# A decoder layer in one kernel: dots that read tokens from SBUF, squares of the norms summed on three engines, and a later hand-over of the low halves

## The chip, the cores and the metric

The kernel runs on one core of one Trainium2 chip. The metric is the device time of one execution in microseconds. Three runs of the kernel before took 3889.0 to 3893.97 us, with a median of 3889.63.

## What is computed

One layer on x with 512 tokens and 2048 channels, in float32. The reference, cut:

```python
proj = x @ w_in[i]
y_conv = conformer_conv(a_conv, ...)      # GLU, causal depthwise conv(31), LayerNorm over 1024, silu, matmul
y_attn = diff_attention(q, k, v, ...)     # 8 heads
mixed = gates[:, :, 0] * y_conv + gates[:, :, 1] * y_attn
x = layer_norm(ALPHA * x + mixed @ w_out[i], ln1_g[i], ln1_b[i])
x = layer_norm(ALPHA * x + peer(x, ...), ln2_g[i], ln2_b[i])
x = x + sigmoid(x @ w_pg + b_pg) * (p[i] @ w_p)
```

and in `peer`, for each token and each of 8 heads, 16 of 16384 experts are picked by product keys:

```python
u = u_tab[ids]
v = v_tab[ids]
h = gelu(einsum('td,thkd->thk', xb, u))
w = (g * h)
return einsum('thk,thkd->td', w, v)
```

## The kernel before

**Layout.** Activations lie transposed: partitions are channels within a chunk of 128, the free axis is tokens. Every large product is a matmul of a 128 x 128 weight tile with 512 (or 352) token columns. To keep float32 accuracy each operand is split in a high half of the type fp32r and a low half, and `three` (lines 655 to 659) issues three matmuls: high x high, low activation x high weight, high activation x low weight.

**Weights.** They come as 784 blocks of 128 x 1024 (512 KB), two of which are a unit. SyncE loads them into four buffers `raw`, ScalarE copies each to `whi` (`hi_part`, L1031) once TensorE is done with the block four before it (AHEAD = 4), and a third engine makes `wlo = raw - whi`: GpSimd in `lo_part` (L570) or VectorE in `lo_part` (L1606). TensorE's `one_block` waits on `lo_done` and then issues 24 matmuls. A raw buffer is loaded again when its low half is made.

**Stages, in blocks.** Heads and gates (B1, B1T), branch outputs (B2), w_out (B3), norm 1, expert queries (B4, 32 blocks), the expert-up loop U5 (B5, 256 blocks, 64 steps of 4), the expert-down loop U6 (B6, 256 blocks), norm 2, and the last projections (B7, B8).

**Two ways through the experts.** For tokens 0 to 351 the kernel runs all 16384 experts densely (352 columns, TU) and keeps the gates in DRAM (`expert_spill`), which is zeroed first and then written one gate per partition by scattered writes: `put_gate` (L592), 384 of them, each after `sum_gate` on VectorE (L1628) has summed the gates of equal experts. For the last 160 tokens it gathers the picked rows: 160 rows per partition of `u_tab` (`gather_u`, L612) and then of `v_tab` (L638), 1 MB for each gather, into a ring of four buffers. `put_gates(n)` stands behind gather n in GpSimd's program, 2.56 writes for each n from 6 on. The first 32 rows (NXP) belong to 32 extra tokens, four times over the partitions. VectorE takes the dot of a gathered row with the token: `extra_dot` (L1619) for the first 32 against `x1e` in SBUF, and `dot` (L1612) for the other 128 against `quad` in PSUM, where TensorE has put the last 128 tokens by sixteen transposes.

**The order on VectorE.** Before the expert-up loop it does the top-16 searches and the routing (decode, weights, offsets). During the first PRE = 7 steps of the loop it is still in its routing and GpSimd makes the low halves, up to DVE_LO = B5 + 4 * PRE. Then VectorE waits for `lo_done` of DVE_LO, makes two lows ahead (LEAD) and runs six `expert_tile`s of 32 blocks: a low, the gate sums, and in three of four blocks a dot. What is left is `POST_DOTS`: 16 dots in the first 20 of 36 blocks.

**The norms.** `norm` on VectorE subtracts the mean of each chunk, `norm_squares` on ScalarE (L1047) squares it into one of two buffers, and `norm_var` on TensorE (L700) sums the squares over partitions and chunks with a matrix of ones: 8 for the conv norm, 16 each for norms 1 and 2. ScalarE waits for the sum of two squares earlier before it writes a buffer again. After the last one ScalarE takes the root (L1050), VectorE the reciprocal, and the chunks are scaled one by one. For the conv norm this stands in TensorE's program behind block 7 of B1T, with blocks 8 to 15 behind it.

Of the kernel before, what the change touches and what calls it, by code (L numbers as in the profile page):

```python
# [18 lines left out]
P = 128  # L19
# [3 lines left out]
ALU = mybir.AluOpType  # L23
# [54 lines left out]

PRE = 7

# [45 lines left out]
def build(nc, ws, xT, pT, cpar, pvec, lamT, keysT, u_tab, v_tab, out):  # L126
# [6 lines left out]
    with ExitStack() as ctx:  # L133
# [28 lines left out]

        x1e = at("x1e", o_ahi, [P, KD, T])

        urows = at("urows", o_s, [P, RING, D])
# [73 lines left out]
        c[0] = o_phase  # L239
        sq = small("sq", [P, 2, T])  # L240
        std = small("std", [P, T])
# [4 lines left out]
        c[0] = o_after_ln  # L246
        gl = small("gl", [P, 2, 2, T])
        mt = small("mt", [P, T])
        xr = small("xr", [P, 2, T])

# [56 lines left out]

        msum2 = at("msum2", o_after_ln, [P, T])
        o_p = c[0]
        c[0] = o_p  # L310
# [53 lines left out]

        ln = [{n: sem(f"{n}{i}") for n in ("mean", "cent", "sqr", "sqr_used", "std_ok", "scaled", "affine", "hi_ok", "lo_ok", "sum")} for i in range(3)]

# [23 lines left out]
        x1e_full = sem("x1e_full")  # L390
        x1e_ok = sem("x1e_ok")
        xsrc_ok = sem("xsrc_ok")
        xg_in = sem("xg_in")
# [152 lines left out]
        def _(pool):  # L546
# [26 lines left out]
            def lo_parts(first, n):  # L573
                with pool.Fori(0, n // 4) as i:
                    for s in range(4):
                        lo_part(4 * i + (first + s), s)

            def spread_picks():

                pool.wait_ge(xsrc_ok, 1)  # L580
                for j in range(NJ):
                    pool.dma_start(xg[j * NX:(j + 1) * NX], xsrc[P - NX:P, :, j * NXP:(j + 1) * NXP]
                                   ).then_inc(xg_in, 16)
# [57 lines left out]

            lo_parts(0, DVE_LO)
            spread_picks()
# [5 lines left out]
            pool.wait_ge(lo_done, B7)  # L649
            lo_parts(B7, NB - B7)  # L650


        @block.tensor
        def _(pe):
# [41 lines left out]
            def norm_var(i, n):  # L696
                for k in range(n):

                    pe.wait_ge(ln[i]["sqr"], k + 1)
                    mm = pe.matmul(ps_o[:], ones[:], sq[:, k % 2], start=(k == 0), stop=(k == n - 1))  # L700
                    mm.then_inc(ln[i]["sqr_used"], 1)

# [94 lines left out]
            for n in range(2 * U1T):  # L797
# [9 lines left out]
                if n == 7:  # L807
                    norm_var(0, NH)

# [214 lines left out]
        def _(act):  # L1024
# [13 lines left out]
            def norm_squares(i, n, src):  # L1038

                act.activation(std[:, 0:1], eps[:], ACT.Sqrt)  # L1040
                for k in range(n):

                    act.wait_ge(ln[i]["cent"], k + 1)
                    if k >= 2:

                        act.wait_ge(ln[i]["sqr_used"], k - 1)
                    act.activation(sq[:, k % 2], src[:, k], ACT.Square).then_inc(ln[i]["sqr"], 1)  # L1047

                act.wait_ge(ln[i]["sqr_used"], n)
                act.activation(std[:], ps_o[:], ACT.Sqrt, bias=eps[:], scale=1.0 / (n * P)  # L1050
# [171 lines left out]
            act.copy(x1e[:, :, TD:T], quad[:].rearrange("p (k d) -> p k d", k=KD)).then_inc(x1e_ok, 1)  # L1222
            with act.Fori(1, SOFT) as i:
                expert_step(i)
# [99 lines left out]
        def _(dve):  # L1324
# [89 lines left out]
            def norm(i, n, src, after):  # L1414
                dve.drain().then_inc(ln[i]["sum"], 1)
                dve.wait_ge(ln[i]["mean"], 1)
                for k in range(n):
                    dve.scalar_tensor_tensor(src[:, k], ps_x[:], -1.0 / (n * P), src[:, k],
                                             ALU.mult, ALU.add).then_inc(ln[i]["cent"], 1)
                dve.wait_ge(ln[i]["std_ok"], 1)  # L1420
                dve.reciprocal(rstd[:], std[:])
# [187 lines left out]
            def dot(n, m, s):  # L1609

                dve.wait_ge(rows_in[s], 16 * m + 16)
                dve.scalar_tensor_tensor(urows[:, s], urows[:, s], 1.0, quad[:], ALU.mult, ALU.mult,  # L1612
                                         accum_out=hd[:, bass.ds(n, 1)]).then_inc(rows_used, 1)
# [40 lines left out]
            dve.wait_ge(x1e_ok, 2)  # L1654
            dve.wait_ge(x1t_full, 1)

# [223 lines left out]
```

## Time and profile before

| | |
|---|---|
| median of 3 runs | 3889.63 us |
| profiled execution | 3876.91 us |
| its span, first to last instruction | 3875.1 us |
| TensorE matmul busy | 3708.9 us (96%) |
| VectorE busy | 2570.0 us (66%) |
| GpSimd busy | 1653.4 us (43%) |
| ScalarE busy | 1296.8 us (33%) |
| mean granted clock of TensorE | 0.976 |
| DMA | 873.53 MB, 225 GB/s over the span |

Busy time is the sum of an engine's instructions; for a stretch of the span the same is given with the clock that TensorE was granted there. A bracket behind an instruction tells how long its engine was idle before it and what ended that. PE is TensorE, PEld its weight loads, ACT ScalarE, DVE VectorE, POOL GpSimd, SP SyncE. Times of instructions are counted from the start of the span.

### The profile page before, as it was taken

Reading aid. Unit: us, or ns where it says so; the run is one execution under the profiler, and the core shown is the slowest. Engines: PE = TensorE matmul, PEld = TensorE weight load, DVE = VectorE, ACT = ScalarE, POOL = GpSimd, SP = SyncE. Lnnn points to the kernel's source line nnn. Section 1 sums busy time; section 2 is a strip of 40 time slices with the busy share of each in tenths; the row PEclk is TensorE's granted clock in tenths of the full one; section 3 lists DMA queues with packets and bytes.
Section 4 is the critical chain, followed back from the end, with each engine's and each line's share of the span. In section 5 each row is a group of like instructions: output and inputs, shape, how many; then the busy total and the mean of one; then the engine's idle time right before and its main releaser. Section 6 shows DMA issues by size and latency. Waiting matters only on the chain.

```text
span 3875.1 us, 56496 instructions
## 1 busy us (share of the span) xinstructions
PE 3708.9 (96%) x19704; PEld 3339.5 (86%) x19704; DVE 2570.0 (66%) x4070; ACT 1296.8 (33%) x1665; POOL 1653.4 (43%) x1032
## 2 busy tenths in 40 slices
PE   8999999999998999898999988999999999999999
PEld 6888888878886889897888887889999999999777
DVE  3555555544413679866777776756999999999732
ACT  4443334441213324343322222223333333333442
POOL 4444444434443336586666565521332222223143
PEclk9999999999999999898999998999999999999999
DMA  5433343324433224788888787877999999999332
GB/s 187 130 125 127 125 129 125 124 98 139 152 121 100 83 91 149 278 298 293 302 313 290 274 301 269 283 261 276 380 385 363 354 362 352 360 358 348 126 111 74
DMA packets 245800, 873.53 MB, mean 225 GB/s; under 512 B 35600, under 2 KB 76752, under 8 KB 204624
## 3 DMA queue, kind: packets, MB, share of 16 engines
q1 hardware_dynamic: 154864, 496.64, 38.1%
q0 software_dynamic: 59360, 340.13, 23.2%
q10 hardware_dynamic: 31488, 35.66, 2.5%
q8 instruction: 47, 0.77, 0.1%
q14 instruction: 41, 0.34, 0.0%
HBM read 813.38 MB, written 58.90 MB: 225 GB/s over the span
## 4 chain that ended last, share of the span: by engine, by line
PE 82%; DVE 7%; issue 4%; POOL 4%; DVEq 2%; ACT 1%; DMA 1%; ACTq 0%; SPq 0%; POOLq 0%
PE bank L657 26%; PE bank L659 26%; PE bank L658 26%; POOL expert_spill L592 3%; DVE yx L1720 2%; PE quad L700 1%; DVE sc L1393 1%; DVE pick L1558 1%; POOL urows L612 1%; DVE wlo L1606 1%; PE bank L719 1%; DVEq L1559 1%; DVEq L1682 0%; PE quad L747 0%; PE bank L858 0%
## 5 line engine op out<-in xcount | busy, mean ns | idle before, releaser
L657 PE MATMUL bank<-ahi,whi 128*128 128x352 f32 (+1 forms) x3968 | 1446.3, 364 | 85.3 <-issue 33.9
L1031 ACT ACTIVATE whi<-raw 128x1024 fp32r<-128x1024 f32 x784 | 827.3, 1058 | 2078.6 <-PE bank L659 1294.9
L659 PE MATMUL bank<-ahi,wlo 128*128 128x352 f32 (+1 forms) x3968 | 1433.9, 361 | 28.8 <-issue 27.7
L658 PE MATMUL bank<-alo,whi 128*128 128x352 f32 (+1 forms) x3968 | 1432.4, 361 | 29.0 <-issue 27.7
L570 POOL TENSOR_TENSOR wlo<-raw,whi 128x1024 fp32r<-128x1024 f32 x304 | 752.0, 2477 | 1056.8 <-ACT whi L1031 1044.0
L657 PEld LDWEIGHTS bank<-ahi,whi 128*128 128x128 f32 x3968 | 763.0, 192 | 191.3 <-issue 78.4
L659 PEld LDWEIGHTS bank<-ahi,wlo 128*128 128x128 f32 x3968 | 762.8, 192 | 122.7 <-issue 45.0
L658 PEld LDWEIGHTS bank<-alo,whi 128*128 128x128 f32 x3968 | 762.7, 192 | 114.3 <-issue 42.0
L1606 DVE TENSOR_TENSOR wlo<-raw,whi 128x1024 fp32r<-128x1024 f32 x484 | 590.1, 1220 | 281.5 <-ACT whi L1031 211.7
L657 PE MATMUL bank<-xwhi,whi 128*128 128x352 f32 x2048 | 661.4, 323 | 1.3 <-DVE xwlo L1692 0.6
L658 PE MATMUL bank<-xwlo,whi 128*128 128x352 f32 x2048 | 656.2, 320 | 0.0
L659 PE MATMUL bank<-xwhi,wlo 128*128 128x352 f32 x2048 | 656.2, 320 | 0.0
L592 POOL DMA_INDIRECT expert_spill<-gval,goff x384 | 431.6, 1124 | 140.0 <-issue 115.2
L638 POOL DMA_INDIRECT vrows<-v_tab,idx x128 | 205.4, 1605 | 547.5 <-DVE yacc L1708 491.8
L657 PEld LDWEIGHTS bank<-xwhi,whi 128*128 128x128 f32 x2048 | 384.1, 188 | 2.7 <-DVE wlo L1606 1.5
L658 PEld LDWEIGHTS bank<-xwlo,whi 128*128 128x128 f32 x2048 | 385.1, 188 | 0.0
L659 PEld LDWEIGHTS bank<-xwhi,wlo 128*128 128x128 f32 x2048 | 384.0, 187 | 0.0
L1612 DVE SCALAR_TENSOR_TENSOR urows<-urows,quad 128x2048 f32<-128x2048 f32 x128 | 292.1, 2282 | 9.2 <-DMA urows<-u_tab,idx 4.9
L1708 DVE SCALAR_TENSOR_TENSOR yacc<-vrows,hd,yacc 128x2048 f32<-128x2048 f32 x116 | 273.4, 2357 | 25.0 <-issue 23.6
L1393 DVE SCALAR_TENSOR_TENSOR sc<-glu,cur,sc 128x512 f32<-128x512 f32 x232 | 270.2, 1165 | 17.3
L612 POOL DMA_INDIRECT urows<-u_tab,idx x128 | 155.4, 1214 | 207.3 <-DVE urows L1612 173.8
L1243 ACT ACTIVATE xwhi<-wt 128x352 fp32r<-128x352 f32 x120 | 59.8, 498 | 336.7 <-DVE wt L1687 329.5
(231 smaller groups left out, 2596.2 us busy)
## 6 DMA issues: line engine op xcount, KB each, us to landing
raw<-ws SPq DMA_DIRECT2D x788, 512.0 KB
hg<-expert_spill SPq DMA_DIRECT2D x58, 704.0 KB, 9.2
expert_spill<-zero SPq DMA_DIRECT2D x32, 704.0 KB, 5.9
expert_spill<-hst ACTq DMA_DIRECT2D x128, 176.0 KB
gate_spill<-gout ACTq DMA_DIRECT2D x32, 256.0 KB, 2.0
gl<-gate_spill SPq DMA_DIRECT2D x32, 256.0 KB, 2.7
expert_spill<-gval,goff POOLq DMA_INDIRECT x384
hg<-expert_spill POOLq DMA_DIRECT2D x6, 704.0 KB, 4.7
```

The lines of the kernel that those rows point to most:

```text
L570: nc.gpsimd.tensor_tensor(wlo[:, s], raw[:, s // 2, s % 2], whi[:, s].bitcast(F32), ALU.subtract).then_inc(lo_done, 1)
L592: nc.gpsimd.indirect_dma_start(eg_flat, bass.IndirectOffsetOnAxis(ap=goff[here, a, n:n + 1], axis=0), gval[here, a, n:n + 1], None).then_i ...
L612: nc.gpsimd.indirect_dma_start(urows[:, n % RING], None, u_tab, bass.IndirectOffsetOnAxis(ap=at_col, axis=0)).then_inc(rows_in[n % RING], 16)
L638: nc.gpsimd.indirect_dma_start(vrows[:, n % RING], None, v_tab, bass.IndirectOffsetOnAxis(ap=at_col, axis=0)).then_inc(rows_in[n % RING], 16)
L657: pe.matmul(ps_out, hi, xh, start=first, stop=False)
L658: pe.matmul(ps_out, hi, xl, start=False, stop=False)
L659: return pe.matmul(ps_out, lo, xh, start=False, stop=last)
L1031: act.activation(whi[:, s], raw[:, s // 2, s % 2], ACT.Copy).then_inc(hi_done, 1)
L1393: dve.scalar_tensor_tensor(dst, glu[:, w:w + T], cur[:, w:w + 1], acc, ALU.mult, ALU.add)
L1606: dve.tensor_tensor(wlo[:, s], raw[:, s // 2, s % 2], whi[:, s].bitcast(F32), ALU.subtract).then_inc(lo_done, 1)
L1612: dve.scalar_tensor_tensor(urows[:, s], urows[:, s], 1.0, quad[:], ALU.mult, ALU.mult, accum_out=hd[:, bass.ds(n, 1)]).then_inc(rows_used, 1)
L1708: dve.scalar_tensor_tensor(yacc[:], vrows[:, s], w, yacc[:], ALU.mult, ALU.add).then_inc(rows_used, 1)
```

## The change

Three edits. PRE goes from 7 to 8. The tokens of the dots are copied from PSUM to `x1t` in SBUF by ScalarE after step 1 of the expert-up loop, and `dot` reads them there. The squares of norms 1 and 2 go in turn to `sqe`, whose column sums TensorE still takes, and to `sqo`, which GpSimd adds up in `sqsum` (`sum_squares`, between two stretches of its low halves); TensorE takes one column sum of that at the end. For the conv norm VectorE adds up all eight squares, and TensorE takes one column sum (`conv_var`).

```diff
-PRE = 7
+PRE = 8
...
+        x1t = at("x1t", o_alo, [P, KD, T])
...
+            def sum_squares(i, n):
+
+                for k in range(1, n, 2):
+                    pool.wait_ge(ln[i]["sqr"], k + 1)
+                    this = sqo[i][:, k // 2 % 2]
+                    if k == 1:
+                        ad = nc.gpsimd.tensor_copy(sqsum[i][:], this)
+                    else:
+                        pool.drain()
+                        ad = nc.gpsimd.tensor_tensor(sqsum[i][:], sqsum[i][:], this, ALU.add)
+                    ad.then_inc(ln[i]["sqr_sum"], 1)
...
-            lo_parts(0, DVE_LO)
+            lo_parts(0, B4 + AHEAD)
+            sum_squares(1, KD)
+            lo_parts(B4 + AHEAD, DVE_LO - B4 - AHEAD)
...
             pool.wait_ge(lo_done, B7)
-            lo_parts(B7, NB - B7)
+            lo_parts(B7, AHEAD)
+            sum_squares(2, KD)
+            lo_parts(B7 + AHEAD, NB - B7 - AHEAD)
...
             def norm_var(i, n):
-                for k in range(n):
+                for k in range(0, n, 2):
 
                     pe.wait_ge(ln[i]["sqr"], k + 1)
-                    mm = pe.matmul(ps_o[:], ones[:], sq[:, k % 2], start=(k == 0), stop=(k == n - 1))
-                    mm.then_inc(ln[i]["sqr_used"], 1)
+                    pe.matmul(ps_o[:], ones[:], sqe[:, k // 2 % 2], start=(k == 0), stop=False
+                              ).then_inc(ln[i]["sqr_used"], 1)
+                pe.wait_ge(ln[i]["sqr_sum"], n // 2)
+                pe.matmul(ps_o[:], ones[:], sqsum[i][:], start=False, stop=True).then_inc(ln[i]["sqr_used"], 1)
+
+            def conv_var():
+
+                pe.wait_ge(ln[0]["sqr_sum"], NH)
+                pe.matmul(ps_o[:], ones[:], sqsum[0][:], start=True, stop=True).then_inc(ln[0]["sqr_used"], 1)
...
                 if n == 7:
-                    norm_var(0, NH)
+                    conv_var()
...
                     act.wait_ge(ln[i]["cent"], k + 1)
-                    if k >= 2:
-
-                        act.wait_ge(ln[i]["sqr_used"], k - 1)
-                    act.activation(sq[:, k % 2], src[:, k], ACT.Square).then_inc(ln[i]["sqr"], 1)
-
-                act.wait_ge(ln[i]["sqr_used"], n)
+                    if i == 0 and k >= 2:
+                        act.wait_ge(ln[i]["sqr_sum"], k - 1)
+                    elif k >= 4:
+                        act.wait_ge(ln[i]["sqr_sum" if k % 2 else "sqr_used"], k // 2 - 1)
+                    to = sqe[:, k % 2] if i == 0 else (sqo[i] if k % 2 else sqe)[:, k // 2 % 2]
+                    act.activation(to, src[:, k], ACT.Square).then_inc(ln[i]["sqr"], 1)
+
+                act.wait_ge(ln[i]["sqr_used"], 1 if i == 0 else n // 2 + 1)
...
-            with act.Fori(1, SOFT) as i:
+            expert_step(1)
+
+            act.wait_ge(x1t_full, 1)
+            act.copy(x1t[:, :, TD:T], quad[:].rearrange("p (k d) -> p k d", k=KD)).then_inc(x1t_ok, 1)
+            with act.Fori(2, SOFT) as i:
                 expert_step(i)
...
+                if i == 0:
+                    for k in range(n):
+                        dve.wait_ge(ln[i]["sqr"], k + 1)
+                        if k == 0:
+                            ad = dve.tensor_copy(sqsum[0][:], sqe[:, 0])
+                        else:
+                            dve.drain()
+                            ad = dve.tensor_tensor(sqsum[0][:], sqsum[0][:], sqe[:, k % 2], ALU.add)
+                        ad.then_inc(ln[i]["sqr_sum"], 1)
                 dve.wait_ge(ln[i]["std_ok"], 1)
...
-                dve.scalar_tensor_tensor(urows[:, s], urows[:, s], 1.0, quad[:], ALU.mult, ALU.mult,
+                rows = urows[:, s].rearrange("p (k d) -> p k d", k=KD)
+                dve.scalar_tensor_tensor(rows, rows, 1.0, x1t[:, :, TD:T], ALU.mult, ALU.mult,
                                          accum_out=hd[:, bass.ds(n, 1)]).then_inc(rows_used, 1)
...
-            dve.wait_ge(x1t_full, 1)
+            dve.wait_ge(x1t_ok, 1)
```

On GpSimd, this is the place between the loop of the low halves and the gathers, before (the four rows in front are the end of that loop, whose count is not in them):

```order
L570 TENSOR_TENSOR wlo<-raw,whi 128x1024
L574 REGISTER_ALU
L574 COMPARE_AND_BRANCH
L582 DMA xg<-xsrc 32x2x32 x4
L612 DMA urows<-u_tab,xg 128x2048 x7
L592 DMA expert_spill<-gval,goff 11534336x1 x3
```

and now (L576 is the low half, L590 and L593 are `sum_squares` for norm 1, L600 the picks, L630 a gather, L610 a scattered write):

```order
L576 TENSOR_TENSOR wlo<-raw,whi 128x1024
L580 REGISTER_ALU
L580 COMPARE_AND_BRANCH
L590 COPY sqsum_155<-sqo_152 128x512
L593 TENSOR_TENSOR sqsum_155<-sqsum_155,sqo_152 128x512 x7
L580 UNCONDITIONAL_BRANCH
...
L576 TENSOR_TENSOR wlo<-raw,whi 128x1024
L580 REGISTER_ALU
L580 COMPARE_AND_BRANCH
L600 DMA xg<-xsrc 32x2x32 x4
L630 DMA urows<-u_tab,xg 128x2048 x7
L610 DMA expert_spill<-gval,goff 11534336x1 x3
```

The loop is cut in two around one copy and seven adds, and the second part runs to four blocks later before the picks and gathers.

On VectorE, the conv norm before:

```order
L1418 SCALAR_TENSOR_TENSOR conv<-quad,conv 128x512 x8
L1421 RECIPROCAL rstd<-std 128x512
L1428 TENSOR_TENSOR nrm<-conv,rstd 128x512 x2
L1436 TENSOR_TENSOR swlo<-conv,swhi 128x512
```

and now:

```order
L1453 SCALAR_TENSOR_TENSOR conv<-quad,conv 128x512 x8
L1459 COPY sqsum_154<-sqe 128x512
L1462 TENSOR_TENSOR sqsum_154<-sqsum_154,sqe 128x512 x7
L1465 RECIPROCAL rstd<-std 128x512
L1472 TENSOR_TENSOR nrm<-conv,rstd 128x512 x2
L1480 TENSOR_TENSOR swlo<-conv,swhi 128x512
```

A copy and seven adds came between the centring of the eight chunks and the reciprocal.

## Rows read from the trace of the kernel before

**Rows 1.** Stretches: busy time and count of each engine, granted clock, DMA share, GB/s.
```profile
core 0: us, PE busy (x) PEld busy (x) DVE busy (x) ACT busy (x) POOL busy (x), PEclk, DMA share, GB/s
1658.00:1758.00 100.00, 91.05 (x541) 89.31 (x541) 70.63 (x134) 41.24 (x44) 82.63 (x58) 0.97 0.89 299
1758.00:2552.00 794.00, 698.79 (x3836) 655.82 (x3835) 541.87 (x1019) 213.08 (x254) 474.03 (x442) 0.91 0.83 289
```

**Rows 2.** Timeline of POOL before the hand-over: start, length, instruction, idle before.
```profile
1530.30 2.39 POOL L570 TENSOR_TENSOR wlo<-raw,whi 128x1024 fp32r<-128x1024 f32 x1 [1.38 <-ACT whi L1031]
...
1545.77 2.39 POOL L570 TENSOR_TENSOR wlo<-raw,whi 128x1024 fp32r<-128x1024 f32 x1 [1.21 <-ACT whi L1031]
...
1552.92 1.04 POOL L612 DMA_INDIRECT urows<-u_tab,xg  x1 [2.38 <-DMA xg<-xsrc]
```

**Rows 3.** Timeline of PE at the hand-over.
```profile
1577.87 0.66 PE L657 MATMUL bank<-ahi,whi 128*128 128x352 f32 x1 [17.82 <-DVE wlo L1606]
```

**Rows 4.** Timeline of DVE behind the last dot.
```profile
2582.59 1.23 DVE L1606 TENSOR_TENSOR wlo<-raw,whi 128x1024 fp32r<-128x1024 f32 x1 [0.16 <-ACT whi L1031]
...
2598.06 1.23 DVE L1606 TENSOR_TENSOR wlo<-raw,whi 128x1024 fp32r<-128x1024 f32 x1 [2.55 <-ACT whi L1031]
```

**Rows 5.** Timeline of DVE and POOL: a dot from SBUF, one from PSUM.
```profile
1653.86 2.29 DVE L1619 SCALAR_TENSOR_TENSOR urows<-urows,x1e 128x2048 f32<-128x2048 f32 x1 [3.26 <-DMA urows<-u_tab,xg]
1653.92 3.08 POOL L592 DMA_INDIRECT expert_spill<-gval,goff  x1 [0.30 <-issue]
...
1772.34 2.28 DVE L1612 SCALAR_TENSOR_TENSOR urows<-urows,quad 128x2048 f32<-128x2048 f32 x1
1773.03 0.97 POOL L592 DMA_INDIRECT expert_spill<-gval,goff  x1 [0.30 <-issue]
```

**Rows 6.** Instructions of one line: least, median and greatest ns.
```profile
L1222 ACT COPY x1e<-quad x1: 1870/1870/1870, 1465.7 to 1465.7; 128x2048 f32<-128x2048 f32 x1
L1468 DVE TENSOR_TENSOR msum<-msum,res x15: 691/691/693, 1075.1 to 1227.5; 128x512 f32<-128x512 f32 x15
```

**Rows 7.** POOL by groups, 1658 to 1758 and 1758 to 2552: busy, mean ns, idle.
```profile
L592 POOL DMA_INDIRECT expert_spill<-gval,goff x41 | 66.5, 1622 | 12.5 <-issue 12.5
L612 POOL DMA_INDIRECT urows<-u_tab,xg x16 | 16.8, 1048 | 4.9 <-issue 4.9
...
L592 POOL DMA_INDIRECT expert_spill<-gval,goff x317 | 324.2, 1023 | 119.6 <-issue 94.7 <-DMA expert_spill<-gval,goff 20.9 <-DVE same L1628 3.9
L612 POOL DMA_INDIRECT urows<-u_tab,idx x125 | 151.6, 1213 | 200.7 <-DVE urows L1612 167.2 <-issue 33.6
```

**Rows 8.** Timeline of POOL: gathers 8, 16, 24, 32 and 156.
```profile
1604.67 2.34 POOL L612 DMA_INDIRECT urows<-u_tab,xg  x1 [0.30 <-issue]
...
1657.30 0.97 POOL L612 DMA_INDIRECT urows<-u_tab,xg  x1 [0.30 <-issue]
...
1708.38 0.97 POOL L612 DMA_INDIRECT urows<-u_tab,xg  x1 [0.30 <-issue]
...
1757.95 0.97 POOL L612 DMA_INDIRECT urows<-u_tab,idx  x1 [0.30 <-issue]
...
2551.78 1.95 POOL L612 DMA_INDIRECT urows<-u_tab,idx  x1 [0.66 <-issue]
```

**Rows 9.** The matches for the gate writes: least, median and greatest ns.
```profile
L1628 DVE SCALAR_TENSOR_TENSOR same<-gflat,gone x384: 227/292/354, 1580.2 to 2524.8; 128x16 f32<-128x16 f32 x24, 128x32 f32<-128x32 f32 x24, 128x48 f32<-128x48 f32 x24, 128x64 f32<-128x64 f32 x24
```

**Rows 10.** Timeline of ACT: first squares and std of conv norm, norm 1, norm 2.
```profile
819.80 1.14 ACT L1047 ACTIVATE sq<-conv 128x512 f32<-128x512 f32 x2
...
830.20 0.69 ACT L1050 ACTIVATE std<-quad,eps 128x512 f32<-128x512 f32 x1 [1.22 <-PE quad L700]
...
1230.18 1.23 ACT L1047 ACTIVATE sq<-res 128x512 f32<-128x512 f32 x2 [0.99 <-DVE res L1418]
...
1246.22 0.69 ACT L1050 ACTIVATE std<-quad,eps 128x512 f32<-128x512 f32 x1 [1.22 <-PE quad L700]
...
3644.25 1.23 ACT L1047 ACTIVATE sq<-res 128x512 f32<-128x512 f32 x2 [5.32 <-DVE res L1418]
...
3661.91 0.69 ACT L1050 ACTIVATE std<-quad,eps 128x512 f32<-128x512 f32 x1 [1.22 <-PE quad L700]
```

More of the change, by code:

```diff
@@ L239, in build @@
         c[0] = o_phase
-        sq = small("sq", [P, 2, T])
+        sqe = small("sqe", [P, 2, T])
         std = small("std", [P, T])
@@ L247, in build @@
         gl = small("gl", [P, 2, 2, T])
+        o_mt = c[0]
         mt = small("mt", [P, T])
+        o_xr = c[0]
         xr = small("xr", [P, 2, T])
@@ L308, in build @@
         msum2 = at("msum2", o_after_ln, [P, T])
+        sqo = [sqe, at("sqo1", o_xr, [P, 2, T]), at("sqo2", o_after_ln + 4 * KB, [P, 2, T])]
+        sqsum = [at("sqsum0", o_mt, [P, T]), at("sqsum1", o_mt, [P, T]), at("sqsum2", o_after_ln + 2 * KB, [P, T])]
         o_p = c[0]
@@ L363, in build @@
         gate_out = [sem(f"gate_out{i}") for i in range(2)]
-        ln = [{n: sem(f"{n}{i}") for n in ("mean", "cent", "sqr", "sqr_used", "std_ok", "scaled", "affine", "hi_ok", "lo_ok", "sum")} for i in range(3)]
+        ln = [{n: sem(f"{n}{i}") for n in ("mean", "cent", "sqr", "sqr_used", "sqr_sum", "std_ok", "scaled", "affine", "hi_ok", "lo_ok", "sum")} for i in range(3)]
         evac2 = sem("evac2")
@@ L391, in build @@
         x1e_ok = sem("x1e_ok")
+        x1t_ok = sem("x1t_ok")
         xsrc_ok = sem("xsrc_ok")
```

## The prediction

> **What bounds the kernel now.** The busy shares come first: TensorE is busy 96% of the span, so a gain must come from stretches where it is not. The stretch table by time finds them. From 1758 to 2552 us, where 124 of the 160 expert rows per token are gathered, TensorE is busy 699 of 794 us at a granted clock of 0.91 and DMA is at 0.83 [rows 1]. That is the expert-up loop (256 weight blocks of 352 columns). Beside each block VectorE makes the low half, and beside three of four blocks it makes one dot of a gathered row, while GpSimd issues 2.56 scattered gate writes for each gather. Two things are to be seen ahead of it. VectorE is still busy with the routing when it has to take over the low halves: GpSimd's lows come every 3.87 us (four in 1545.77 - 1530.30 = 15.47 us) and stop with block 27 [rows 2]; TensorE then stands 17.8 us for VectorE's first low [rows 3]. And at each of the three layer norms TensorE does little: 16 us of squares and column sums, one bound to the next.
>
> **Part 1, PRE 7 to 8.** GpSimd keeps four more low halves (blocks 28 to 31 of the loop). The routing on VectorE is not touched and ends at the same 1576.6. TensorE does these four blocks in 15.5 us of its 17.8 us of standing, and waits about 2.4 us instead. The gain stays if what follows keeps its rate: dots are bound to blocks by the program, all of it shifted by four blocks, so that at the last dot (about 2580 us) 12 blocks are left, not 16. Blocks without dots go at 3.87 us (2582.59 to 2598.06 for four [rows 4]): **-15.5 us**. GpSimd's first gather has to wait for its last low, some 15.5 us later than 1552.9 [rows 2], so 1568.4; VectorE waits for the picks that come before that gather, and is still in its routing until 1576.6. The first two gathers have 8 us left to land. I cost this at nothing; if that cover were gone, it would cost the few us by which the picks are late.
>
> **Part 2, dots from SBUF.** The dot does not get faster: 2.29 us with x1e in SBUF, 2.28 with the tokens in PSUM [rows 5]. The added ScalarE copy is like the one of x1e, 1.87 us [rows 6], beside three blocks of prepared weights: nothing. What changes is GpSimd. With an SBUF dot on VectorE, an indirect DMA that starts 0.06 us behind the dot takes 3.08 us; in a PSUM dot one takes 0.97 [rows 5]. The first 32 dots already read SBUF, so the kernel before shows both. In the stretch with SBUF dots a scattered write takes 1.622 us on average and GpSimd is never idle but for 0.30 us of issue; afterwards 1.023 us, and GpSimd waits 167 us for dots [rows 7]. So GpSimd loses its slack of 167 us and becomes the engine that sets the pace of the loop. How fast? From gather 16 to gather 32 (1657.30 to 1757.95) 6.29 us each; from 32 to 156 (to 2551.78), 6.40 each [rows 8]. The other way round, the 442 instructions of that stretch at the SBUF prices are 317 x 1.622 + 125 x 1.048 + 442 x 0.30 = 778 us, against 794 now. The matches that VectorE does for the gate writes also hold SBUF, and grow from 0.23 to 0.35 us over the loop [rows 9], 2.56 of them for each gather: on average of the later rows 0.055 us wider than in the measured stretch, so at most 0.14 us a gather or 17 us in all, and I take half, 9. That makes 787: **-7 us**. Why a slower GpSimd need not lengthen the loop: now it runs ahead at 1.28 us a transfer whenever a buffer comes free, then waits; VectorE waits for weights in that stretch while TensorE stands. Bounds: 778 with no growth (-16); the whole SBUF window (gather 8 to 32, 153.3 us, 6.39 each) with all the growth, 792 + 17 (+15).
>
> The Trainium skill, page "SBUF — State Buffer", section "Who interferes with whom", says that a VectorE instruction with two SBUF inputs contends with a GpSimd instruction that reads SBUF, but infers that descriptor generation is left alone, as it needs the write interface. Here the indirect DMAs, which read their indices from SBUF, do stretch, so the trace agrees with the first half and speaks against the second. By the second half alone part 2 would be worth nothing and the time 3866.
>
> **Part 3, the norms.** Conv norm: the squares start at 819.80 and the std at 830.20 [rows 10], because the eight column sums wait behind block 7. Now VectorE adds: an add of this size is 0.69 us [rows 6], 0.77 with the drain, so the eighth is in at about 820.4 + 0.5 + 7 x 0.77 = 826.3, and with 1.2 us for the one column sum std starts at 827.5: -2.7. TensorE now stands about 3.5 us there; should the clock fall, it eats this. I take -2.5. Norm 1: 1230.18 to 1246.22, 16.0 us; norm 2: 3644.25 to 3661.91, 17.7 us [rows 10]. Now ScalarE can go at its 0.62 us a square (two in 1.23), 10 us in all, TensorE sums the even ones, and GpSimd adds the odd ones. Its add is not in the trace. Below: half the 2.39 us of its low of twice the size [rows 2], 1.2, and with drain and semaphore 1.4, so 1.3 + 0.9 + 7 x 1.4 + 1.2 = 13.2 us. Above: 2.4 us each regardless of size, 22 us. A tensor operation of the same kind is most likely in proportion; I take 13.9 us. That is -2.1 and -3.8, and the recipes behind (reciprocal, scaling) are unchanged. TensorE has nothing queued but the blocks that need this norm. **-8.4 us**; if GpSimd's add cost 2.4 us each, norms 1 and 2 would give +10 instead of -6.
>
> **Sum:** -15.5 - 7 - 8.4 = **-31 us**. Against the profiled execution (3876.9, span 3875.1) 3846; against the median of the three timed runs, 12.7 us above it, **3859**. I carry the same difference over to the median.
>
> **Rivals.**
> 1. *GpSimd's pace is worse than the loop's now* (slower). Deciding point: the gains besides it are 24 us, so 124 gathers must take over 818 us, 6.59 us each. For it: eight gathers of the SBUF stretch took 6.58 (1604.67 to 1657.30); against it: the next eight 6.39, the next 6.20, falling [rows 8]. At 6.58 and with the whole 17 us of growth, 833: +39, in all 3889.6 - 24 + 39 = 3905. 10%.
> 2. *Given back* (same): 6.58 without growth is 816, +22, leaving 3888; or GpSimd's adds at 2.4 us, 3875, with some of the pace lost too. 10%.
> 3. *No contention felt* (faster, by the part 2 that is worth nothing): the ring of four buffers already hid GpSimd, the loop stays at 6.40 a gather: -24, 3866. 15%.
> 4. *The loop runs more evenly* (faster): the last eight SBUF gathers took 6.20; 124 at that are 769, -25 in place of -7, and the stalls of TensorE between 1758 and 2552 fall away: 3841. 15%.
> That the change does not do what it says is excluded for the dots and lows, which are plain in the order; for the norms it would be rival 2.
>
> **Numbers.** The forecast has 50%. Faster by over 0.2% (7.8 us, about what a measurement of this kernel tells from no change) holds with the forecast and rivals 3 and 4 and the better part of rival 2's second half: 0.81. Same 0.10, slower 0.09. The range leaves out rival 1 and the far end of 4: 3838 to 3889.
>
> **What would show it.** TensorE's stand at the takeover 2 to 4 us, not 17.8. GpSimd's scattered writes at 1.6 us on average through the whole loop, its wait for dots near zero, gathers 6.2 to 6.5 us apart. From the first square to std 7.7, 13.9 and 13.9 us. The prediction is wrong if gathers are over 6.59 us apart, if TensorE stands over 10 us at the takeover for another reason (picks late), or if a sum on GpSimd takes over 2 us.

## The result and the profile after

| | before | change |
|---|---|---|
| median of 4 runs | 3889.32 us | 3837.77 us |
| lowest and highest | 3877.72, 3893.97 | 3833.62, 3845.64 |
| profiled execution | 3876.91 us | 3838.33 us |
| mean granted clock | 0.976 | 0.985 |

The ratio is 0.9874, 95% interval 0.9847 to 0.9901: 51.6 us by the medians, 38.6 us by the two profiled executions. The forecast was 3859, faster, with a range from 3838; the median lies 0.2 us below its low end. This is the result beside one set of runs of the kernel before. Beside another set (2, below) the change is slower than before by 3.6%; the experiments come to that.

The page after, its span, busy shares and chain (before, the chain had PE 82% and POOL 4%):

```profile
span 3836.5 us, 56450 instructions
PE 3656.1 (95%) x19662; PEld 3320.2 (87%) x19662; DVE 2581.6 (67%) x4074; ACT 1301.0 (34%) x1668; POOL 1827.5 (48%) x1052
...
PE 63%; POOL 19%; DVE 7%; issue 5%; DVEq 2%; DMA 1%; ACT 1%; ACTq 0%; POOLq 0%; SPq 0%
```

The loop's two stretches after, gather 16 to 32 (1661.7 to 1762.6) and gather 32 to 156, in the columns of [rows 1]:

```profile
1663.00:1763.00 100.00, 93.27 (x556) 91.82 (x555) 70.00 (x136) 41.86 (x44) 82.63 (x58) 0.97 0.91 300
1763.00:2541.00 778.00, 674.46 (x3951) 656.00 (x3950) 553.07 (x1023) 219.92 (x261) 617.45 (x442) 0.96 0.88 298
```

The same 442 instructions of GpSimd that took 474 us of 794 now take 617 of 778. The groups of GpSimd and VectorE in that second stretch (compare [rows 7]):

```profile
L610 POOL DMA_INDIRECT expert_spill<-gval,goff x317 | 476.7, 1504 | 122.7 <-issue 95.1 <-DMA expert_spill<-gval,goff 24.1 <-DVE same L1673 3.6
L630 POOL DMA_INDIRECT urows<-u_tab,idx x125 | 141.8, 1135 | 38.1 <-issue 38.1
...
L1657 DVE SCALAR_TENSOR_TENSOR urows<-urows,x1t 128x2048 f32<-128x2048 f32 x123 | 281.9, 2292 | 206.0 <-DMA urows<-u_tab,idx 164.3 <-issue 41.3
```

GpSimd never waits for a dot any more (167 us before). The wait has changed sides: VectorE's dots now wait 164 us for gathered rows (4.9 us before). GpSimd sets the pace.

The hand-over after, on GpSimd, TensorE's weight loads and VectorE (compare [rows 2] and [rows 3]):

```profile
1560.04 2.40 POOL L576 TENSOR_TENSOR wlo<-raw,whi 128x1024 fp32r<-128x1024 f32 x1 [1.48 <-ACT whi L1060]
1562.38 2.44 POOL L600 DMA_DIRECT2D xg<-xsrc  x4
1567.30 1.04 POOL L630 DMA_INDIRECT urows<-u_tab,xg  x1 [2.48 <-DMA xg<-xsrc]
...
1585.15 0.29 PEld L679 LDWEIGHTS bank<-ahi,whi 128*128 128x128 f32 x1 [11.11 <-DVE wlo L1650]
...
1583.85 3.51 DVE L1650 TENSOR_TENSOR wlo<-raw,whi 128x1024 fp32r<-128x1024 f32 x3 [0.31 <-issue]
```

TensorE still stands 11.1 us by its loads, 10.8 by its matmuls (17.8 before), not 2 to 4. VectorE takes over at 1583.85; before it did at 1576.6. Where those 7.3 us come from, two groups of VectorE's routing show, of before from 1545 to 1577:

```profile
L1549 DVE SCALAR_TENSOR_TENSOR term<-pij,know 128x256 f32<-128x256 f32 x30 | 11.4, 421 | 1.1
L1558 DVE TENSOR_TENSOR pick<-pick,term 128x256 f32<-128x256 f32 x30 | 11.4, 421 | 1.5 <-issue 0.4
```

and of after from 1545 to 1584:

```profile
L1602 DVE TENSOR_TENSOR pick<-pick,term 128x256 f32<-128x256 f32 x30 | 20.0, 706 | 1.1
L1593 DVE SCALAR_TENSOR_TENSOR term<-pij,know 128x256 f32<-128x256 f32 x30 | 11.4, 422 | 1.5 <-issue 0.4
```

The thirty adds of `pick`, with two inputs in SBUF, grew by 8.6 us in all. They now lie beside four more low halves of GpSimd. A low half, and two adds of which the first lies beside it:

```profile
1556.17 2.39 POOL L576 TENSOR_TENSOR wlo<-raw,whi 128x1024 fp32r<-128x1024 f32 x1 [1.38 <-ACT whi L1060]
...
1556.36 2.81 DVE L1602 TENSOR_TENSOR pick<-pick,term 128x256 f32<-128x256 f32 x2
```

Only four adds grew: each began 0.05 to 0.3 us behind one of the four low halves, ended just behind it, and took 2.48 to 2.63 us; the others stayed near 0.42. The instructions of `term`, which also read two tensors in SBUF, did not grow: none of them began while a low half ran. The one of the same line that writes `pick` did begin behind one in both kernels, and took 2.48 us before and 2.62 after.

**The account.** These are marks in the two traces, after minus before, with what each stretch gave in brackets: first low half of the expert-up loop -1.1 us; third gather +7.2 (1583.8 against 1576.6; +8.3, the hand-over's loss); gather 32 +4.6 (-2.6); gather 156 -11.1 (-15.7); last dot -20.9 (2559.2 against 2580.1, -9.8); first low of the down loop -40.4 (2608.2 against 2648.6, -19.5); end -38.6 (+1.8).

### The profile page after: what moved, and what is told of

Read it like the earlier page. It is cut to its first block, busy times and chain, and to the rows that moved or that the text cites. A ratio compares the mean times of both kernels' runs of the same rounds, so it can differ in the third digit from the quotient of the medians.

```text
span 3836.5 us, 56450 instructions
## 1 busy us (share of the span) xinstructions
PE 3656.1 (95%) x19662; PEld 3320.2 (87%) x19662; DVE 2581.6 (67%) x4074; ACT 1301.0 (34%) x1668; POOL 1827.5 (48%) x1052
## 4 chain that ended last, share of the span: by engine, by line
PE 63%; POOL 19%; DVE 7%; issue 5%; DVEq 2%; DMA 1%; ACT 1%; ACTq 0%; POOLq 0%; SPq 0%
PE bank L679 20%; PE bank L681 20%; PE bank L680 20%; POOL expert_spill L610 15%; POOL urows L630 4%; DVE yx L1765 2%; DVE sc L1428 1%; DVEq L1603 1%; DVE pick L1602 1%; DMA expert_spill<-gval,goff 1%; DVE wlo L1650 1%; PE bank L748 1%; DVEq L1727 0%; PE quad L776 0%; DMA urows<-u_tab,idx 0%
## 5 line engine op out<-in xcount | busy, mean ns | idle before, releaser
L576 POOL TENSOR_TENSOR wlo<-raw,whi 128x1024 fp32r<-128x1024 f32 x308 | 764.5, 2486 | 1024.7 <-ACT whi L1060 1011.7
L610 POOL DMA_INDIRECT expert_spill<-gval,goff x384 | 579.4, 1509 | 143.2 <-issue 115.5
L1657 DVE SCALAR_TENSOR_TENSOR urows<-urows,x1t 128x2048 f32<-128x2048 f32 x128 | 293.3, 2292 | 210.5 <-DMA urows<-u_tab,idx 168.5
L630 POOL DMA_INDIRECT urows<-u_tab,idx x128 | 145.4, 1136 | 40.8 <-issue 38.7
```

Source lines behind the costliest of these rows:

```text
L576: nc.gpsimd.tensor_tensor(wlo[:, s], raw[:, s // 2, s % 2], whi[:, s].bitcast(F32), ALU.subtract).then_inc(lo_done, 1)
L610: nc.gpsimd.indirect_dma_start(eg_flat, bass.IndirectOffsetOnAxis(ap=goff[here, a, n:n + 1], axis=0), gval[here, a, n:n + 1], None).then_i ...
L630: nc.gpsimd.indirect_dma_start(urows[:, n % RING], None, u_tab, bass.IndirectOffsetOnAxis(ap=at_col, axis=0)).then_inc(rows_in[n % RING], 16)
L1657: dve.scalar_tensor_tensor(rows, rows, 1.0, x1t[:, :, TD:T], ALU.mult, ALU.mult, accum_out=hd[:, bass.ds(n, 1)]).then_inc(rows_used, 1)
```

## The experiments

All times are medians; "before" is the kernel before, run in the same set. A set of runs shares one chip. There were five sets after the result, each with a number here, and the kernel before falls on two levels in them, which are called the lower (3714 to 3718) and the upper (3871 to 3889, the result's own set among them):

| set | kernels | before |
|---|---|---|
| 1 | b_again, b_pre8, b_x1t, b_norms | 3870.6 (3856.3 to 3886.7, 29 runs) |
| 2 | after_again, a_psum, a_paced, a_pre9 | 3718.4 (3701.3 to 3723.2, 13 runs) |
| 3 | a_psum_2, a_ring3 | 3713.9 (3705.1 to 3721.1, 19 runs) |
| 4 | a_half | 3716.1 (3706.1 to 3717.7, 7 runs) |
| 5 | a_psum9 | 3879.2 (3866.4 to 3890.2, 13 runs) |

### The kernel before, unchanged

> The kernel before, unchanged, for its spread. Theory (GpSimd's bursts): the expert-up loop's pace depends on how transfers collide, so the gathers' pace should differ from execution to execution: 6.40 us a gather in the profile of before (3876.9), about 6.5 where an execution takes 3889. Rival: the 12 us between that profile and the median lie anywhere, and the pace is 6.40 again.

Measured 3869.04, ratio 0.9995 [0.9977, 1.0013]. The same program, built again, gives the same time. Gathers 32 to 156 came 6.38 us apart in an execution of 3879, so the theory's 6.5 did not come and the rival's 6.40 did.

### One part alone

```diff
-PRE = 7
+PRE = 8
```

> Before with PRE = 8 alone. Theory (the longer low halves on GpSimd block VectorE's routing): the routing ends 7 to 9 us later, TensorE stands some 11 us at the hand-over, the time falls by 7 to 10 us. Rival (the routing was late by chance): it ends at the old time, TensorE stands 2 to 3 us, -15.5 us.

Measured 3861.84, ratio 0.9974 [0.9954, 0.9994], -9 us. The third gather came at 1588.5 (1577.2 in b_again, whose lows ran 2.5 us earlier); TensorE stood 11.0 us. So the late routing belongs to this part, and it brings what is left of 15.5 us after it. The profiled execution, 3841.91, was the quickest of its ten, and its gathers came 6.20 us apart, so its trace is not that of its median, and the pace of the loop with dots from PSUM is perhaps less steady than b_again alone would say.

```diff
+            act.copy(x1t[:, :, TD:T], quad[:].rearrange("p (k d) -> p k d", k=KD)).then_inc(x1t_ok, 1)
...
-                dve.scalar_tensor_tensor(urows[:, s], urows[:, s], 1.0, quad[:], ALU.mult, ALU.mult,
+                dve.scalar_tensor_tensor(rows, rows, 1.0, x1t[:, :, TD:T], ALU.mult, ALU.mult,
```

> Before with the dots from SBUF alone (and the copy). Theory (the held port keeps GpSimd from bursting, and the loop runs evenly): writes 1.5 us on average, gathers 6.27 us apart, TensorE's clock in the loop up from 0.91 to 0.96, -25 us against the profile of before, up to -38 against its median. Rival (nothing gained here, the gain of the change came from the other two parts): -7 us or less.

Above is the main part of the edit; it also moves ScalarE's step 1 out of its loop, as in the change. Measured 3850.59, ratio 0.9936 [0.9914, 0.9959], -20 us: the largest part by itself. Gathers 32 to 156 came 6.26 us apart. In its groups from 1763 to 2400 GpSimd's writes are as slow as in the change:

```profile
L594 POOL DMA_INDIRECT expert_spill<-gval,goff x264 | 397.2, 1505 | 90.0 <-issue 79.8 <-DMA expert_spill<-gval,goff 10.1
L659 PE MATMUL bank<-ahi,whi 128*128 128x352 f32 x1098 | 368.8, 336 | 75.4 <-DVE wlo L1612 75.1
```

The norms alone (the `sqe`, `sqo`, `sqsum`, `sum_squares` and `conv_var` lines of the diff):

> Before with the new sums of squares alone. Theory (TensorE, left with less work, falls to the low clock, and GpSimd is late in norm 2): -1 to -3 us in all. The forecast: -8.4 us. In norm 2 GpSimd's first add comes 4.8 us late if that is a fixed property of the program, and about 0.2 us late if it was chance.

Measured 3871.53, ratio 0.9994 [0.9972, 1.0015]: nothing that can be told. In its profile, from first square to std: 9.0, 13.7 and 17.7 us (10.4, 16.0 and 16.0 in b_again beside it). GpSimd's first add of norm 2 is 4.8 us late here too.

The three parts alone add up to some 28 us. The change took 51.6 off the medians of its own set and 33 off this set's; its whole was not run in this set, so whether the parts help each other is not shown.

### The change again, and the source of the dots undone

> The change, unchanged, as the base of this group: about 0.990 of the kernel before, the routing late and TensorE's stand at the hand-over 10.8 us again (a fixed property), GpSimd's first add of norm 2 late by 4.8 us again or not.

Measured 3848.82 with before at 3718.4: ratio 1.0358 [1.034, 1.0375], **slower** by 130 us. No theory expected that. But the change itself hardly moved: its four times, 3834 to 3852, overlap with the result's 3834 to 3846, gathers 32 to 156 came 6.25 us apart (6.28 in the result), and TensorE's stand at the hand-over was 10.8 us again. What moved is the kernel before.

```diff
-                dve.scalar_tensor_tensor(rows, rows, 1.0, x1t[:, :, TD:T], ALU.mult, ALU.mult,
+                dve.scalar_tensor_tensor(urows[:, s], urows[:, s], 1.0, quad[:], ALU.mult, ALU.mult,
```

> The change with the dots read from PSUM again (the copy to SBUF stays and is not read). Theory (GpSimd's bursts): gathers 6.3 to 6.5 us apart, DMA uneven, 15 to 25 us slower than the change. Rival (the even pace does not matter): within 5 us of it.

Measured 3708.24, ratio 0.9975 [0.9961, 0.999]; 141 us under the change, by the source of the dots alone. Gathers came 5.17 us apart. It was run again in set 3:

> The changed kernel with its dots reading PSUM again (the copy is made all the same), a second time, beside a new set of the kernel before. If this chip is of the kind on which the kernel before takes 3856 to 3894: theory 1 (the dots from SBUF bring the larger part of the gain there, as b_x1t against before, some 20 us) expects 3852 to 3862, gathers 6.2 to 6.4 us apart and TensorE with issue gaps inside blocks of the up loop. Theory 2 (the hand-over and the norms bring it and the source of the dots is worth nothing) expects 3835 to 3845. If the chip is of the kind on which before takes 3718: 3708 again, gathers 5.17 us apart and no such gaps.

Measured 3703.57, ratio 0.9972 [0.9957, 0.9986]. Its stretch from 1763 to 2400 (columns as in [rows 1]), and its matmul and GpSimd groups there:

```profile
1763.00:2400.00 637.00, 632.52 (x3923) 631.33 (x3922) 547.28 (x1021) 218.03 (x260) 468.46 (x440) 1.00 0.98 362
...
L680 PE MATMUL bank<-alo,whi 128*128 128x352 f32 x1308 | 424.3, 324 | 0.0
L679 PE MATMUL bank<-ahi,whi 128*128 128x352 f32 x1307 | 422.3, 323 | 4.5 <-DVE wlo L1650 4.3
L610 POOL DMA_INDIRECT expert_spill<-gval,goff x315 | 335.2, 1064 | 125.1 <-issue 94.2 <-DMA expert_spill<-gval,goff 30.7 <-DVE same L1672 0.3
```

TensorE is busy 632.5 of 637 us at clock 1.00. Three dots go with four blocks at 3.87 us [rows 4], which is 5.16 us a gather: TensorE's own pace. GpSimd's writes are at 1.06 us and leave it room. The same stretch of the kernel before, as it was profiled for the result:

```profile
1763.00:2400.00 637.00, 564.50 (x3126) 531.81 (x3125) 443.46 (x845) 174.53 (x207) 388.34 (x360) 0.92 0.84 293
...
L659 PE MATMUL bank<-ahi,wlo 128*128 128x352 f32 x1042 | 351.9, 338 | 21.8 <-issue 21.0
L657 PE MATMUL bank<-ahi,whi 128*128 128x352 f32 x1042 | 351.6, 337 | 29.4 <-issue 25.8 <-DVE wlo L1606 2.8
```

Here TensorE has "issue" gaps inside blocks: it waits for nothing that the profile shows. Matmuls that follow each other at 0.16 us elsewhere come 0.7 us apart, in clusters mostly 25 to 50 us from each other; one cluster in windows and in PE's timeline:

```profile
1900.00:1904.00 4.00, 4.00 (x27) 4.00 (x26) 3.91 (x8) 1.57 (x3) 3.35 (x3) 1.00 0.53 148
1912.00:1916.00 4.00, 4.00 (x27) 4.00 (x26) 1.44 (x2) 0.76 (x1) 3.09 (x4) 1.00 1.03 410
1916.00:1920.00 4.00, 2.40 (x9) 1.14 (x7) 3.58 (x6) 0.30 (x1) 3.09 (x4) 1.00 0.98 379
1920.00:1924.00 4.00, 2.77 (x8) 1.94 (x9) 0.39 (x2) 0.00 (x0) 3.09 (x4) 0.64 0.82 259
1924.00:1928.00 4.00, 3.41 (x12) 3.24 (x12) 0.32 (x1) 1.41 (x2) 0.80 (x1) 0.51 0.54 203
...
1917.99 0.41 PE L657 MATMUL bank<-ahi,whi 128*128 128x352 f32 x1 [0.39 <-issue]
1918.70 0.32 PE L658 MATMUL bank<-alo,whi 128*128 128x352 f32 x1 [0.30 <-issue]
```

The gaps begin with DMA at its full share; the granted clock falls after them (1.00, 0.64, 0.51), and DMA then drops to half. The gaps (60 to 72 us of 637 in the three matmul lines) are in every profile with dots from PSUM of sets 1 and 5 and in that of the kernel before, and in none of sets 2 and 3. Profiles with dots from SBUF have none, in any set, but for 10.4 us on one matmul line of the change. In windows of 4 us from 1900 to 2020 the DMA share swings between 0.53 and 1.07 before and 0.71 and 1.01 after; in a_psum_2 it stays at 0.81 to 1.09 without any gap, so a full share by itself does not make them. Nor do loads of instructions, by their number: the trace of before has 10 of them in the 637 us, that of a_psum_2 has 13, and the clusters are some 19.

### Is it GpSimd's pace?

```diff
+                    if NXP <= n < 140:
+                        pool.drain()
+                        nc.gpsimd.memset(idle[:], 0.0)
```

> As a_psum (dots from PSUM), but GpSimd writes a scratch tile for some 0.9 us after the gate writes of each gather from 32 to 139, which with issue and drain makes up the 1.3 to 1.4 us that an SBUF dot holds it. Theory (it is GpSimd's pace that counts, not where the dot reads): the time of the change within 5 us, gathers about 6.3 us apart, GpSimd's wait for dots small. Rival (a PSUM read by VectorE slows TensorE, and SBUF is better in itself): the time of a_psum or worse.

Measured 4201.26, ratio 1.1311 [1.129, 1.1333]. It misses its aim: the edit was to cost 0.9 us a gather, and gathers came 9.16 us apart. The group of the added instruction, from 1763 to 2400:

```profile
L639 POOL MEMSET idle<- 128x960 f32 x66 | 59.3, 898 | 259.6 <-issue 259.6
```

259.6/66 = 3.9 us pass before each memset, where the added drain stands behind indirect DMAs. The run says nothing on the theories.

The next edit gives GpSimd half of the load, by reading every second dot from PSUM:

```diff
+                by = x1t[:, :, TD:T]
+                if s % 2:
+                    rows, by = urows[:, s], quad[:]
+                dve.scalar_tensor_tensor(rows, rows, 1.0, by, ALU.mult, ALU.mult,
```

> The changed kernel with every second dot (ring buffers 1 and 3) reading its tokens from PSUM and the others from SBUF. Theory 1 (GpSimd's own time sets the pace, because its indirect DMAs stretch under dots from SBUF; where they do not, TensorE's blocks do): GpSimd needs 3.56 indirect DMAs a gather, at 1.41 us on average and 0.30 us between them with all dots from SBUF (6.1 us, measured 6.25) and at 1.07 us with none (4.9 us, below the 5.16 us of TensorE's four blocks for three dots). With half it needs 5.5 to 5.6, so on a chip where before takes 3718 gathers come 5.5 to 5.65 us apart and the time is 3705 + 124 x 0.4 = 3750 to 3765. Theory 2 (the dots from SBUF cost something else, such as ScalarE's copy or where the buffers lie, not a share per dot): 3838 to 3850 again, or 3705. On a chip where before takes 3850 to 3894, theory 1 expects at least 5.5 us a gather from GpSimd, and what TensorE and the weight transfers take on top of it there is open: 3770 to 3850.

Measured 3776.09, ratio 1.0173 [1.0154, 1.0191]. Gathers came 5.73 us apart, between 5.17 with none and 6.25 with all; the time is the middle of 3704 to 3708 and 3849. GpSimd in this kernel, from 1763 to 2400:

```profile
L610 POOL DMA_INDIRECT expert_spill<-gval,goff x285 | 346.1, 1214 | 106.4 <-issue 85.0 <-DMA expert_spill<-gval,goff 20.8 <-DVE same L1676 0.6
L630 POOL DMA_INDIRECT urows<-u_tab,idx x111 | 151.5, 1365 | 33.8 <-issue 33.2 <-DVE urows L1660 0.6
```

It waits 0.6 us for dots in all, so it sets the pace again, at a write of 1.21 us (1.06 and 1.50 at the ends). Each dot from SBUF costs its share, which is theory 1; the time is 11 us above its upper figure, as the gathers themselves grew to 1.37 us. Theory 2 had one of the old times and is out; the copy is made in a_psum too, which runs at TensorE's pace.

```diff
-                        pool.wait_ge(rows_used, n - RING + 1)
+                        pool.wait_ge(rows_used, n - RING + 2)
```

> The changed kernel with its dots from PSUM and GpSimd allowed one row buffer less ahead in the up loop: each gather waits for rows_used at n - 2, not n - 3, so at most three row buffers are in flight or unread. Theory 1 (the loop is slow with PSUM dots because GpSimd, with time to spare, runs ahead in bursts that crowd the weight transfers, and dots from SBUF only pace it) expects that the tighter ring removes part of this: on a chip where before takes over 3850, gathers 6.3 us apart or less, smaller issue gaps on TensorE than in a_psum_2, and a time 5 to 20 us under a_psum_2. Theory 2 (it is the PSUM read itself that disturbs TensorE) expects the same gaps and the same time as a_psum_2, within 5 us. Theory 3 (the loop needs the whole ring to cover a gather's landing time) expects VectorE to wait for rows, gathers 6.5 us apart or more, and over 20 us above a_psum_2. On a chip where before takes 3718 theories 1 and 2 both expect a_psum_2's time or up to 10 us above it.

Measured 3713.87, ratio 1.0003 [0.9994, 1.0013], 10 us above a_psum_2; gathers 5.22 us apart. The set was at the level without issue gaps, so theories 1 and 2 were not told apart. Theory 3 is out on this level: three buffers nearly do.

### Four blocks more

PRE = 9, in the change and in a_psum:

> The change with PRE = 9. TensorE's stand at the hand-over (10.8 us) goes; the routing ends at the same time or up to 2 us later, since GpSimd's next lows come when it is nearly over; GpSimd's gathers begin 1 to 4 us later than now. The last dot is late by as much, but 8 blocks are left behind it and not 12, 15.5 us. Theory: -11 to -14 us against the change. Rival (the loop's end is bound by the gathers and their start, which are later): 0 to -5 us.

Measured 3838.92, 10 us under after_again (set 2), with four runs each: 3838 to 3843 against 3834 to 3852, so the gain is not clear of the spread, and the two profiled executions go the other way (3842.8 against 3833.9). In them the first gather is at 1581.6 and the third at 1591.1, 8.7 us later: the routing ends later still. TensorE's stand is down to 4.0 us from 10.8. The last dot is 17.0 us later, and 12.0 of the 15.5 us come back behind it.

> Dots from PSUM (the copy is made all the same), the norms of the change, and PRE = 9, four more low halves for GpSimd before the hand-over. Theory 1 (each four blocks moved to GpSimd are worth 15.5 us at the end of the up loop, and cost the 7 to 8 us by which the picks on VectorE end later, and what TensorE then waits for weights): 5 to 10 us under a_psum and a_psum_2, which took 3708 and 3704, so 3694 to 3703 on a chip where before takes 3714 to 3718, and 4 to 6 permille under before. Theory 2 (the hand-over is used up: TensorE stands for VectorE as long as before, since the picks end later still): 3704 to 3712. On a chip where before takes 3850 to 3894: under before by 10 to 25 us, and at or above the change's 3838.

Measured 3870.39 with before at 3879.2, ratio 0.9978 [0.996, 0.9996]. The set fell on the upper level, and this kernel has the issue gaps there. TensorE stands 4.0 us at the hand-over, so theory 2, a stand as long as before, is out. Its stretch and one group, 1763 to 2400:

```profile
1763.00:2400.00 637.00, 560.31 (x3053) 524.16 (x3053) 428.73 (x815) 171.44 (x203) 384.62 (x354) 0.90 0.82 289
...
L680 PE MATMUL bank<-alo,whi 128*128 128x352 f32 x1018 | 346.4, 340 | 31.7 <-issue 31.1
```

All of the change but the dots from SBUF, with PRE = 9 on top, is worth 9 us at this level, and the change's own runs of the other sets, at 3834 to 3852, lie below all ten of its runs (lowest 3861). The gain was expected at 10 to 25 us, so that is a small miss; that the kernel stays above the change was expected.

## Why the prediction was right, and where it was not

**Sign and mechanism, right at the level of its rows.** GpSimd lost its slack and became the engine that sets the pace; that this need not lengthen the loop was the argument of part 2, and the profile after shows it, as does b_x1t alone. Rival 1 needed 6.59 us a gather; it was 6.28. But one of the three signs that the prediction named for being wrong did come: TensorE stood over 10 us at the takeover.

**Part 1, -15.5, with the routing "not touched".** This step failed. The four blocks brought their 15.5 at the end of the loop (-19.5 there, with 4.0 of other gain), but "the routing on VectorE is not touched and ends at the same 1576.6" is wrong: it ended 7.3 us later, since the moved low halves of GpSimd lie beside the adds of `pick`. The 8 us of cover were on the wrong thing, the landing of the gathers. Four adds at 2.5 us in place of 0.42 are the price; b_pre8 has four such adds and a_pre9, with four more low halves, has eight. Net of the 8.3 us lost at the hand-over the part is worth some 7 us, and 9 when run alone.

**Part 2, -7.** From gather 32 to 156 the loop took 778.1 us, the figure of the working before 9 us of growth were added. Part of that is luck: the writes took 1.504 us on average, not 1.622, the gathers 1.135, not 1.048, and 24 us of waits for GpSimd's own earlier write were not in the sum, though [rows 7] had them at 20.9. Not in it either: with GpSimd the slower, dots follow the gathers closely, so the last dot came 18.5 us behind gather 156 and not 28.3 (-9.8), and the start of the loop gave 2.6. In all 28 us against 7, so this term was the one most mis-sized. The rival "the loop runs more evenly" named half of this: TensorE's issue gaps are gone from the stretch but for 10 us, while 6.20 us a gather was not reached. Its 3841 is also nearer to the 3838 measured than the forecast's 3859.

**Part 3, -8.4.** Measured -1.4, -1.0 and +0.1 (conv norm, norms 1 and 2, from the first square to std), against the -2.5, -2.1 and -3.8 that were summed. First, the squares of the conv norm (compare [rows 10]):

```profile
820.76 1.14 ACT L1078 ACTIVATE sqe<-conv 128x512 f32<-128x512 f32 x2
...
829.76 0.69 ACT L1081 ACTIVATE std<-quad,eps 128x512 f32<-128x512 f32 x1 [3.01 <-PE quad L730]
```

The adds went at 0.79 us each, 0.77 reckoned. The last ended at 827.59, and std came 2.2 us later, not 1.2: TensorE, which had stood for them, took 1.22 and 1.06 us for the two halves of the one column sum. Norm 1:

```profile
1230.39 0.63 ACT L1078 ACTIVATE sqe<-res 128x512 f32<-128x512 f32 x1 [1.00 <-DVE res L1453]
...
1233.24 0.63 ACT L1078 ACTIVATE sqe<-res 128x512 f32<-128x512 f32 x1 [0.43 <-PE quad L722]
...
1245.43 0.69 ACT L1081 ACTIVATE std<-quad,eps 128x512 f32<-128x512 f32 x1 [4.04 <-PE quad L725]
...
1230.00:1247.00 17.00, 12.46 (x18) 3.93 (x18) 10.17 (x17) 9.90 (x17) 10.12 (x9) 0.71 0.09 31
```

GpSimd's add is 1.27 us and 1.43 with what lies between, as taken (1.4). TensorE, with 18 matmuls in this stretch in place of 32, was granted 0.71 of its clock (1.2 GHz from 1230.2 to 1237.0); before it was 1.00. Its column sums held up ScalarE (0.43 us before the square at 1233.24). The other profiles of this code price the clock: norm 1 took 13.7 to 13.8 us in five where the clock from 1230.5 to 1237 was 0.74, close to the 13.9 forecast, and 14.8 to 15.1 in five where it was 0.50 to 0.54. Norm 2, on GpSimd:

```profile
3607.08 0.61 POOL L590 COPY sqsum<-sqo 128x512 f32<-128x512 f32 x1 [5.64 <-ACT sqo L1078]
3612.49 1.26 POOL L593 TENSOR_TENSOR sqsum<-sqsum,sqo 128x512 f32<-128x512 f32 x1 [4.80 <-issue]
3613.91 1.27 POOL L593 TENSOR_TENSOR sqsum<-sqsum,sqo 128x512 f32<-128x512 f32 x1 [0.16 <-issue]
```

The first add comes 4.80 us after the copy, waiting for nothing that is shown; all of the expected 3.8 us went there, in every profile of this code (17.7 to 17.8 us). The old code is not steady there either: 17.7 us in the profile of before and 17.6 in b_pre8, 16.0 in b_again and b_x1t. What the 4.80 us are stays open; norm 1, with the same two instructions, does not have them.

**The carry-over.** The sum against the profiled execution gave 3846, and 3838 came. Adding 12.7 us for the median was wrong: that was the place of one execution in the spread of before, 3877 to 3894, and the change has a spread and a place of its own. Errors of both signs nearly cancel in the sum, which is luck: part 2 gave 21 us more than its term, parts 1 and 3 gave 8 and 6 less. That left 8 us, and this 13 then made most of the miss in the median.

**What the prediction did not see.** Its rows of before were of one level. Where before takes 3714 to 3718, the loop with dots from PSUM runs at TensorE's 5.16 us, GpSimd's 6.26 us decide, and the change loses 3.6%: rival 1's mechanism, with its deciding point moved from 6.59 to some 5.36 us (an estimate: 5.17 from a_psum, plus the prediction's other 24 us of gains over 124 gathers). The rows that pointed to it were there: TensorE busy 699 of 794 us at 0.91, with no engine full. The prediction took that as the loop's rate and did not ask what the missing 95 us were.

**On the page of the Trainium skill**, "SBUF — State Buffer", section "Who interferes with whom": the experiments with half and all of the dots bear out its first half, that a VectorE instruction with two SBUF inputs contends with a GpSimd instruction that reads SBUF, also for indirect DMAs (writes of 1.06, 1.21 and 1.50 us). An indirect DMA reads its indices from SBUF, so these runs don't tell whether the generation of its descriptors is touched or only that read; the prediction's "speaks against the second" goes further than they do. The adds of `pick` (0.42 us alone, 2.48 to 2.63 behind a low half) show the same contention from VectorE's side.

**Open.** What sets the level. The records number the chips; number 1 appears in sets 1 and 3, on either level, so the number does not decide it, and within a set no run crosses over. Why TensorE has issue gaps at the upper level and only with dots from PSUM was not settled: the runs show that they come with large swings of the DMA share, and that the gaps are all but gone with GpSimd at 6.26 us a gather, where the share still swings (0.60 to 1.01 in b_x1t from 1900 to 2020); which is the cause isn't shown. No run at the upper level slows GpSimd by other means than the dots, so that it is GpSimd's pace that removes them is not shown either. A ring of three was to test the bursts and fell on the other level.

## What to carry to other kernels

A change that slows an engine with slack is judged by what the loop would run at without its stalls, not by what it runs at now: first account for the idle time of the busiest engine. When work is moved to GpSimd, look on VectorE for instructions with two SBUF inputs beside it, in both directions. Keep a copy of the kernel before in each set of runs, and measure on more than one set before a change of 1% is kept: of the versions run, a_psum is the best on the lower level (3704 to 3708) and the change on the upper (3838), and none is known to be the best on both. The change with PRE = 9 was not run on the upper level, nor was a_psum with PRE = 8.

## What the runs showed of the hardware

- The same program has two levels, 3714 to 3718 and 3871 to 3889 us, kept within a set. The kernel before was not profiled on the lower one; in a_psum and a_psum9, which are alike but for PRE, the difference is in the expert-up loop (5.17 against 6.54 us a gather).
- The change takes 3838 on the upper and 3849 on the lower level (medians of four each, whose ranges overlap).
- In a_paced 3.9 us pass at a drain on GpSimd behind indirect DMAs (mean of 66).
- GpSimd: copy of 128x512 0.61 us, add 1.27 us, 0.16 us between two adds with a drain; 4.80 us between the copy and the first add of norm 2, in every profile of that code.
- An add of 128x256 on VectorE with two SBUF inputs takes 0.42 us alone, and 2.48 to 2.63 when it begins just behind a low half of GpSimd (2.4 to 2.5 us); over the thirty adds that makes 0.71 on average.
- An indirect DMA of GpSimd for one gate write takes 1.06, 1.21 and 1.50 us on average with none, half and all of VectorE's dots reading SBUF.
